# One SSD layer's group loop on one core: decay rows issued ahead of two weight units, and the modulation columns turned into another bank

## The reference, cut to what matters

```python
def ssd_mixer(hx, hc, w_in, conv_w, conv_b, dt_bias, a_log, d_skip, norm_w, w_out):
    ...
        zxbcdt = h @ w_in
        z = zxbcdt[..., :D_INNER]
        xbc = jax.nn.silu(depthwise_conv_same(zxbcdt[..., D_INNER:D_INNER + CONV_CH], conv_w, conv_b))
    ...
        decay = jnp.exp(jnp.where(lower, seg, -jnp.inf))
        cb = jnp.einsum('bign,bjgn->bijg', c_, b_)
        y_intra = jnp.einsum('bijg,bijgr,bjgr,bjgrp->bigrp', cb, decay, dt_, x_)
        y_state = jnp.einsum('bign,bgrpn->bigrp', c_, state) * jnp.exp(acum)[..., None]
    ...
    out = gated_rmsnorm(y, z, norm_w) @ w_out
```

## Time and profile before

| | us |
|---|---|
| median of 3 runs (2265.98 to 2270.43) | 2269.93 |
| the profiled execution | 2270.54 |
| its span, first to last instruction | 2268.7 |
| PE busy in it | 2133.5 |
| DVE busy | 1458.6 |
| ACT busy | 1231.6 |
| POOL busy | 47.8 |

### The profile page before, as it was taken

One profiled execution on the slowest core, in us unless ns is written; L12 is line 12 of the kernel. 1 busy time (PEld: TensorE's weight loads), 2 busy tenths in 40 slices (PEclk: granted clock), 3 DMA queues, 4 the chain that ended last, 5 costly groups with the idle time before them and its releaser, 6 DMA issues.

```text
span 2268.7 us, 27496 instructions
## 1 busy us (share of the span) xinstructions
PE 2133.5 (94%) x11320; PEld 1720.4 (76%) x11320; DVE 1458.6 (64%) x1392; ACT 1231.6 (54%) x1373; POOL 47.8 (2%) x20
## 2 busy tenths in 40 slices
PE   6889999979899999999878999999999999999997
PEld 4677878767677777878567887888878787888875
DVE  3567777753333323225646888878878887888884
ACT  4567666652322222224645767666767676675763
POOL 0011111100000000000000000000000000000000
PEclk9999999979899999999988999999999999999998
DMA  8233445432245444332315999999999999999990
GB/s 305 95 117 145 140 155 181 175 112 75 84 157 174 161 170 160 109 110 96 131 54 213 361 341 339 346 352 331 358 338 345 333 342 345 341 359 335 345 338 21
DMA packets 137732, 509.61 MB, mean 225 GB/s; under 512 B 15296, under 2 KB 15680, under 8 KB 135296
## 3 DMA queue, kind: packets, MB, share of 16 engines
q1 hardware_dynamic: 137520, 507.65, 62.7%
q10 hardware_dynamic: 80, 0.13, 0.0%
HBM read 504.45 MB, written 3.28 MB: 224 GB/s over the span
## 4 chain that ended last, share of the span: by engine, by line
PE 81%; DVE 8%; ACT 4%; issue 1%; DVEq 0%; ACTq 0%
PE ps L1076 14%; PE ps L1074 14%; PE ps L1075 14%; PE ps L654 10%; PE ps L656 10%; PE ps L655 10%; DVE area L1783 3%; DVE d_lo L1654 2%; PE ps L1060 1%; PE ps L1133 1%; ACT area L1315 1%; PE ps L1103 1%; PE ps L666 1%; PE ps L751 1%; ACT d_hi L1247 1%
## 5 line engine op out<-in xcount | busy, mean ns | idle before, releaser
L2102 DVE TENSOR_TENSOR w_lo<-w_raw,w_hi 128x2048 fp32r<-128x2048 f32 x336 | 749.3, 2285 | 51.7 <-ACT w_hi L1537 50.8
L1537 ACT ACTIVATE w_hi<-w_raw 128x2048 fp32r<-128x2048 f32 x336 | 625.8, 1918 | 79.0 <-PE ps L1076 78.2
L1654 DVE TENSOR_TENSOR d_lo<-d_raw,d_hi 128x2048 fp32r<-128x2048 f32 (+1 forms) x76 | 171.9, 2262 | 333.8 <-ACT d_hi L1247 333.8
L1074 PE MATMUL ps<-w_hi,x_hi 128*128 128x512 f32 x896 | 357.1, 399 | 2.0 <-DVE x_lo L2158 2.0
L654 PE MATMUL ps<-h_top,d_hi 128*128 128x512 f32 (+1 forms) x816 | 331.5, 406 | 25.5 <-DVE h_low L1646 9.8
L1076 PE MATMUL ps<-w_hi,x_lo 128*128 128x512 f32 x896 | 355.0, 396 | 0.0
L1247 ACT ACTIVATE d_hi<-d_raw 128x2048 fp32r<-128x2048 f32 (+1 forms) x76 | 143.7, 1890 | 381.8 <-DMA d_raw<-in_dense 244.3
L1075 PE MATMUL ps<-w_lo,x_hi 128*128 128x512 f32 x896 | 350.7, 391 | 0.0
L656 PE MATMUL ps<-h_top,d_lo 128*128 128x512 f32 (+1 forms) x816 | 322.9, 396 | 0.0
L655 PE MATMUL ps<-h_low,d_hi 128*128 128x512 f32 (+1 forms) x816 | 319.3, 391 | 0.0
L654 PEld LDWEIGHTS ps<-h_top,d_hi 128*128 128x128 f32 x816 | 158.3, 194 | 69.9 <-issue 26.2
(11 more groups left out here) (275 smaller groups left out, 2493.2 us busy)
## 6 DMA issues: line engine op xcount, KB each, us to landing
w_raw<-in_experts SPq DMA_DIRECT2D x672, 512.0 KB, 5.6
d_raw<-in_dense SPq DMA_DIRECT2D x240, 512.0 KB, 5.2
area<-acum_rows SPq DMA_DIRECT2D x16, 1024.0 KB, 8.4
d_raw<-in_dense SPq DMA_DIRECT2D x8, 384.0 KB, 4.0
xT<-in_xt SPq DMA_DIRECT2D x4, 512.0 KB, 6.7
gate_rows<-area SPq DMA_DIRECT2D x4, 512.0 KB, 6.8
hT<-gate_rows SPq DMA_DIRECT2D x2, 1024.0 KB, 5.9
cst<-in_consts SPq DMA_DIRECT2D x2, 512.0 KB, 10.9
```

What stands on the lines that cost most here:

```text
L1074: mm(o, hi, w_hi[u % HIGH][:, a:a + 512], start=first, stop=False)
L1537: A(w_hi[n % HIGH][:], w_raw[n % RAW][:], ACT.Copy).then_inc(S["whi_done"], 1)
L1654: TT(d_lo[u][:, 0:w], d_raw[u][:, 0:w], d_hi[si % D_HIGH][:, 0:w].bitcast(F32), ALU.subtract)\
L2102: TT(w_lo[n % RAW][:], w_raw[n % RAW][:], w_hi[n % HIGH][:].bitcast(F32), ALU.subtract)\
```

## The change

It has two parts. The first moves `load_rowb(g)` in SP's queue two units forward: it now stands before `bc` g+1 instead of before `m0` 9+2g, and `load_rowb(7)` stands before `m0` 22 instead of before the second `wout` unit. The second lets `turn_pair` of the loop and its tail write bank 5 in place of bank 4, so that `group_sums` no longer waits for `mod_done`; `group_spread`, which writes bank 5, waits for it now. A wait for `st_op` before the last `turn_pair` goes away.

```diff
@@ SP
-                if unit[0] == "m0" and 8 <= unit[1] < 23 and unit[1] % 2:
-                    load_rowb((unit[1] - 9) // 2)
+                if unit[0] == "bc" and unit[1]:
+                    load_rowb(unit[1] - 1)
+                if unit == ("m0", 22, 0):
+                    load_rowb(7)
                 if unit == ("wout", 1, 0):
-                    load_rowb(7)
                     sp.wait_ge(S["d_used"], D_AT[("z", 7, 0)] + 1)
@@ PE
             def group_sums(g):
 
                 pe.wait_ge(S["ysq_done"], 2 * g + 2)
-                pe.wait_ge(S["mod_done"], 5 + g)
@@
             def group_spread(g):
 
                 pe.wait_ge(S["grinv_done"], g + 1)
+                pe.wait_ge(S["mod_done"], 5 + g)
@@
-                turn_pair(4 + g, 4)
+                turn_pair(4 + g, 5)
@@
             mod_pair(11, 5)
-            pe.wait_ge(S["st_op"], 80)
-            turn_pair(11, 4)
+            turn_pair(11, 5)
@@ DVE, mod_out
-                    TT(modT[:, 0, 4 * p:4 * p + 4, :], ps[4][:, 0:8].rearrange("p (m r) -> p m r", m=4),
+                    TT(modT[:, 0, 4 * p:4 * p + 4, :], ps[5][:, 0:8].rearrange("p (m r) -> p m r", m=4),
```

## The result

The changed kernel takes 2300.57 us (median of 4 runs, 2299.33 to 2301.33) against 2267.95 of the kernel before (median of 4 runs, 2264.78 to 2270.43): a ratio of 1.0142, 95% interval 1.0128 to 1.0156. It is 32.6 us slower, where the sum of the forecast gave 0.2 us. The profiled executions stand at 2299.33 and 2270.54, their spans at 2297.5 and 2268.7.

A forecast was written before the change was run, and what follows sets the result against it. PE holds 81% of the last chain, but the loop's path passes through PE, DVE and ACT. Terms -2.5 + 2.7 = +0.2 on the median 2269.93 gave 2270.1, put at 2270.5 us; range 2266 to 2276.

The forecast's parts named there:

- the term put at nothing for the rows of groups 1 to 6: GpSimd's selects get their rows earlier but end at the same place, behind DVE's convolution; gain 0.
- Rival D: GpSimd's earlier selects stop DVE in the convolution, 2.0 us each, +12 in all: 2282; chance 0.04.
- Rival A: The clock falls at PE's new wait before `bc`, 1.7 us each; 2273.5 to 2275.5, all six 2280.5; chance 0.22.
- The -2.5 of the bank part: Loop over the groups with the turn in bank 5: what clock falls cost beyond the cover comes back, -2.5 us.
- the circle: Path of a group: PE from `bc` to `mod_pair`, DVE's convolution, ACT to its copy of `x`, `bc` again; 49.96 us.
- The first group, +2.7: `bc` 1 lands later behind the rows, so ACT's exponentials start at 110.7 instead of 108.02; bounds 2.0 to 3.5.
- the sums' wait goes: `group_sums` no longer waits for `mod_out` and starts about 1.5 us earlier in each of seven groups.
- the spread's new wait for `mod_done` costs nothing: Cost 0: `mod_out` is done 1.5 us behind the turn, the spread comes some 8 us behind it.
- the `st_op` wait's removal: Before the last turn: gives 0, since that turn waits for `mod_rows`, which DVE runs behind the same `state_ops`.
- `bc` and `m0` land in time in the later groups: Behind the rows in the queue, `bc` has 5 us of slack and `m0` is needed only by `mod_pair`; cost 0.
- rival C: PE alone sets the period, so waits and half clock come off: -17 + 3, 2256; chance 0.03.

The follow-up runs named there:

- e3_gate_end: The changed kernel with GpSimd's selects held until both halves of DVE's convolution are done; 2275.19 us, ratio 1.0027 to the kernel before.
- e5_gate_third: The changed kernel with GpSimd let go one convolution instruction later than in e4_gate_mid, so it asks during the third of eight; 2276.45 us (one run).
- e4_gate_mid: The changed kernel with GpSimd let go after the first of eight instructions of the convolution's second half; 2299.97 us, ratio 1.0134 to the kernel before.
- e1_bank: The changed kernel's bank 5 part alone, decay rows at their old place in the queue; 2274.43 us, ratio 1.0022 to the kernel before.
- e7_fill: e1_bank with useless matmuls in PE's wait before `bc` (8, in pass 0 27); 2263.58 us, ratio 0.9975 to the kernel before.
- e8_fill_row0: e7_fill with the decay rows of group 0 alone moved ahead of `bc` 1; 2269.73 us, ratio 0.9999 to the kernel before.
- e10_mended: e7_fill with the rows of groups 1 to 7 at the new place and GpSimd held until the convolution is done; 2264.26 us, ratio 0.9977 to before.
- e6_taps: e4_gate_mid with the convolution's taps in the order 3, 4, 0, 1 instead of 0, 1, 3, 4; 2300.56 us (one run).

## Why the prediction was wrong

**The step that failed** is the term put at nothing for the rows of groups 1 to 6: "So GpSimd may start at about 350.3", "An earlier start ends at the same place", "Gain 0". The arrival was right: it came 0.4 us ahead of the second half of the convolution, at 370.59 against 371.00, where 350.3 against 350.83 had been foreseen. What it meant was wrong, and the prediction misread its own row: 350.3 isn't "at the start of the same stretch" but half a microsecond before it. I took from 117 unstretched instructions that DVE always wins against a select. Only 48 of them, in six passes, had a select come while their row ran, and it came 1.91 us behind the start of the row at the earliest, in the third instruction. A select that comes before the row, or in its first two instructions, was in no row of before; `e3_gate_end` and `e5_gate_third` against `e4_gate_mid` showed what it costs: 1.75 us for each of two selects, 3.49 a pass, in six passes, 20.9 us.

**Rival D** named this mechanism and the place where it bites, with 2.0 a select and 12 us in all (one select for each of six groups), and 0.04 of the chance. It is what happened, with both selects and 3.49 in each of six groups. The rule of the Trainium skill ("SBUF — State Buffer", section "Who interferes with whom"), that whoever comes first keeps the ports for its instruction, speaks for more of it than I granted; the selects that came first did stop DVE. By that rule alone a select would wait for one DVE instruction, and the traces differ there: one that came at the third instruction waited 3.6 us, through six of them.

**Rival A** happened at the same time: half clock behind the new wait in six of six passes. I had priced it at 1.7 each; 1.65 were measured on average, 1.3 to 1.6 in five periods and 2.8 in the sixth. The two were weighed as alternatives, while a stop of DVE makes the wait before `bc` longer (3.6 instead of 2.2) and the fall surer (18 of 18 places in three traces behind the long wait, 13 of 18 in three behind the short one). Together they are 30.9, and a range that took the rivals one at a time, 2266 to 2276, did not reach there.

**The -2.5 of the bank part** is a second step that failed: it rested on the clock staying up behind the moved wait. In the profiled execution of `e1_bank` it fell at four of six, and the part alone was 5.6 us slower. The mechanism (the wait moves to `bc`, the circle stays at 49.96) was right and is shown by `e7_fill`, which came within 0.2 us of its number.

**The first group, +2.7**: 3.4 to 3.5 measured by the start of the exponentials behind the issue of the rows, at the upper bound given. The term was a little small, and it brings 2.7 of half clock behind it when the rest of the clock is up (`e8_fill_row0`).

Right: the sums' wait goes; the spread's new wait for `mod_done` costs nothing, and no cost of the `st_op` wait's removal shows; `bc` and `m0` land in time in the later groups (`e10_mended`); PE alone doesn't set the period (rival C).

Open: the medians differ by 32.6 us, the two profiled executions by 28.8. Both profiled ones lie at the edge of their runs, the changed one lowest and the one before highest. What the others have more was not looked at.

## What to carry to other kernels

An engine off the critical path still has a moment at which it starts, and an earlier input moves it: before handing GpSimd its data sooner, look at what DVE runs at that moment, and hold the select back by a semaphore if it must not come first. Ask of "never stretched in before" in which positions it was ever tried.

Taking a wait away from PE only moved it to the next dependence here. There it stood in front of work that is on the path, and the half clock behind it cost more than the wait was worth; filling it, and the wait of pass 0, with useless matmuls was worth 10.9 us.

## What wasn't expected of the hardware

A select of GpSimd that came 0.3 us into the second of eight back-to-back DVE instructions got in ahead of the third and its successor ahead of the fourth (2.5 us each instead of 0.74); one that came 0.3 us into the third waited 3.6 us, to the end of the row, and DVE lost nothing. Another order of the taps, which changes the offset of the reads, made no difference in the one run that tried it. So the engines do not meet only at semaphores, as the opening has it: DVE and GpSimd also stop each other, DVE for 3.49 us a pass in the changed kernel.

The granted clock fell to 1.2 GHz in `bc` in four, four and five of six places behind a wait of 2.2 us (`e1_bank`, `e3_gate_end`, `e5_gate_third`), in six of six behind one of 3.6 (the changed kernel, `e4_gate_mid`, `e6_taps`), and in none when all but 0.4 us of it was filled with matmuls (`e7_fill`).
